# The first modulated norm in four blocks instead of two, and ten row tiles of the fourth modulation segment on ScalarE and GpSimd instead of six of the third on VectorE

## What is computed

```python
silu_c = jax.nn.silu(c)                                   # c: (1, 2048)
mod = silu_c @ w_ada[l] + b_ada[l]                        # w_ada: 2048 x 12288
shift_m, scale_m, gate_m, shift_f, scale_f, gate_f = jnp.split(mod, N_MOD, axis=-1)
h = modulate(rmsnorm(x, g_norm_mix[l]), shift_m, scale_m) # h * (1 + scale) + shift
proj = h @ w_in[l]                                        # queries, keys, values, latents
dq, dk, dv, q_lat, kv_lat, k_pe = jnp.split(proj, IN_SPLITS, axis=-1)
```

## Time and profile before

| | |
|---|---|
| median of 3 runs | 2601.45 us (2601.24 to 2601.49) |
| time of the profiled execution | 2600.53 us |
| its span | 2598.9 us |
| TensorE busy | 2526.1 us, 97% |
| VectorE busy | 1936.0 us, 74% |
| ScalarE busy | 1135.2 us, 44% |
| GpSimd busy | 175.8 us, 7% |
| chain that ended last | TensorE 80%, VectorE 8%, DMA 6%, issue 2%, ScalarE 2% |
| mean DMA rate | 253 GB/s |
| slices 1 to 3 of 40 (65 us each) | TensorE 5, 9, 9 tenths busy; 374, 370, 364 GB/s |

### The profile page before, as it was taken

How to read it: one execution, slowest core, us unless ns; L and a number is a source line. 1 busy time by engine, 2 the same in 40 slices (tenths; PEclk the granted TensorE clock), 3 DMA queues, 4 the chain that set the end, 5 groups by cost and what they waited for, 6 DMA issues and landing times.

```text
span 2598.9 us, 45233 instructions
## 1 busy us (share of the span) xinstructions
PE 2526.1 (97%) x17210; PEld 2274.1 (88%) x17210; DVE 1936.0 (74%) x2037; ACT 1135.2 (44%) x1326; POOL 175.8 (7%) x288
## 2 busy tenths in 40 slices
PE   5999999999999999999999999999989999999998
PEld 3787789788999998998999999999969898898986
DVE  2476598778788887889878988888777566575665
ACT  2334444444444444444334444544454444444443
POOL 6000000200001010110000000001010000000000
PEclk8999999999999999999999999999999999999999
DMA  9998868688889887886877765678847676676764
GB/s 374 370 364 291 268 216 291 203 284 303 291 291 311 287 297 252 303 300 194 265 219 235 235 219 158 186 246 280 284 141 254 207 241 226 212 246 211 225 219 138
DMA packets 304432, 658.63 MB, mean 253 GB/s; under 512 B 31351, under 2 KB 37646, under 8 KB 303918
## 3 DMA queue, kind: packets, MB, share of 16 engines
q1 hardware_dynamic: 271376, 538.12, 61.0%
q0 software_dynamic: 32480, 117.56, 13.7%
q10 hardware_dynamic: 446, 1.13, 0.1%
HBM read 654.62 MB, written 2.10 MB: 253 GB/s over the span
## 4 chain that ended last, share of the span: by engine, by line
PE 80%; DVE 8%; DMA 6%; issue 2%; ACT 2%; SPq 0%; ACTq 0%; DVEq 0%
PE ps L2106 19%; PE ps L2107 10%; PE ps L2077 9%; PE ps L2078 9%; PE ps L2079 9%; PE ps L2154 6%; PE ps L2156 6%; PE ps L2155 6%; DMA raw<-in_w_ff 3%; DVE lo L1161 3%; DMA proj<-in_w_ada 1%; DMA raw<-in_w_in 1%; DVE work L1186 1%; ACT hi L717 1%; PE ps L2323 1%
## 5 line engine op out<-in xcount | busy, mean ns | idle before, releaser
L1161 DVE TENSOR_TENSOR lo<-raw,hi 128x1024 fp32r<-128x1024 f32 (+2 forms) x868 | 1036.8, 1210 | 516.5 <-ACT hi L717 513.4
L717 ACT ACTIVATE hi<-raw 128x1024 fp32r<-128x1024 f32 (+2 forms) x868 | 901.6, 1049 | 1166.0 <-PE ps L2079 391.9
L2106 PE MATMUL ps<-acts,hi 128*128 128x512 f32 x2048 | 673.9, 383 | 9.1 <-DVE lo L1161 6.7
L2077 PE MATMUL ps<-acts,hi 128*128 128x256 f32 x2384 | 668.4, 280 | 9.2 <-issue 2.7
L2078 PE MATMUL ps<-acts,hi 128*128 128x256 f32 x2384 | 658.8, 276 | 0.0
L2079 PE MATMUL ps<-acts,lo 128*128 128x256 f32 x2384 | 658.8, 276 | 0.0
L2107 PE MATMUL ps<-acts,lo 128*128 128x256 f32 x2048 | 558.7, 273 | 0.0
L2077 PEld LDWEIGHTS ps<-acts,hi 128*128 128x128 f32 x2384 | 458.6, 192 | 41.2 <-issue 33.7
L2078 PEld LDWEIGHTS ps<-acts,hi 128*128 128x128 f32 x2384 | 458.7, 192 | 0.7 <-issue 0.2
L2079 PEld LDWEIGHTS ps<-acts,lo 128*128 128x128 f32 x2384 | 458.9, 192 | 0.2
L2106 PEld LDWEIGHTS ps<-acts,hi 128*128 128x128 f32 x2048 | 387.3, 189 | 67.3 <-DVE lo L1161 9.5
(11 more groups left out here) (308 smaller groups left out, 2437.2 us busy)
## 6 DMA issues: line engine op xcount, KB each, us to landing
raw<-in_w_ff SPq DMA_DIRECT2D x512, 512.0 KB, 4.7
raw<-in_w_in SPq DMA_DIRECT2D x232, 512.0 KB, 4.6
ada_ring<-in_w_ada POOLq DMA_DIRECT2D x150, 512.0 KB, 5.4
proj<-in_w_ada SPq DMA_DIRECT2D x92, 512.0 KB, 8.3
proj<-in_w_ada POOLq DMA_DIRECT2D x64, 512.0 KB, 5.3
ada_ring<-in_w_ada SPq DMA_DIRECT2D x40, 512.0 KB, 6.5
raw<-in_w_out SPq DMA_DIRECT2D x32, 512.0 KB, 5.6
raw<-in_w_o SPq DMA_DIRECT2D x32, 512.0 KB, 5.6
```

What stands on the lines that cost most here:

```text
L717: nc.scalar.activation(hi[n % SPLIT][:, 0:k], raw[n % RAW][:, 0:k], ACT.Copy).then_inc(hi_ready, 1)
L1161: V.tensor_tensor(lo[n % SPLIT][:, 0:k], raw[n % RAW][:, 0:k], hi[n % SPLIT][:, 0:k].bitcast(F32), ALU.subtract)\
L2077: M(out, h, right_hi, start=start, stop=False)
L2106: M(out[:, j, :], h[:, t, js], both, start=k == 0, stop=False)
```

## The change

`BLOCKS` and `OPEN` become 4. A block is now 512 columns of the shift and of the scale together, 8 block tiles, each of which brings 512 columns of both segments; `turn_block` makes both at once with two-column matmuls, and `finish_block` writes both. Only block 0 stands ahead of the first chunk. Each block has 8 chunks: four groups of 512 columns, with two chunks (4 k tiles) each. A group's partial sum leaves PSUM after its two chunks: VectorE copies it into `proj` in block 0 (L1521) and adds it there in the others (L1524), 16 passes of 128x1024. The 8 tiles of the next block stand behind the chunks 0 to 4 of a block, its turn behind chunk 5.

22 pairs are left, between chunks 24 and 62: all of segment 2, and the last 6 row tiles of segment 3. The first ten row tiles of segment 3 come as twenty halves. Each is loaded behind chunk 37 + h, scaled in place by ScalarE behind the split that stands at chunk 33 + h, and added by GpSimd. The load of half h waits until half h - 4 was added. `sum_halves` stands in `kvlat`. Rotations of keys and queries are cut differently: two of 4 tiles and one of 2 in `qk1`, three of 2 in `v1` (before: three of 4 and two of 2).

```diff
-OPEN = 3
-BLOCKS = 2
+OPEN = 4
+BLOCKS = 4
-HALVES = 12
+HALVES = 20
...
-        tiles_after = {1: (0,), 2: (1, 2), 3: (3,), 4: (4, 5), 5: (6,), 6: (7, 8), 7: (9, 10), 8: (11, 12), 9: (13, 14, 15)}
-        half_lo = (16, 18, 19, 21, 22, 24, 29, 30, 32, 33, 34, 35)
+        tiles_after = {0: (0, 1), 1: (2,), 2: (3, 4), 3: (5,), 4: (6, 7)}
+        TURN_AFTER = 5
+        pair_after = {(24 + 21 * p // 15 if p < KT else 47 + 15 * (p - KT) // (KT - MOVED - 1)): p for p in range(2 * KT - MOVED)}
+        halves_after = {33 + h: (h,) for h in range(HALVES)}
...
@@ SyncE
-                    sp.dma_start(start_ring[n % START][t], w_ada[0][row:row + P, col:col + 2 * NC]).then_inc(start_landed[n % START], 16)
+                    both = w_ada[0][row:row + P, 0:2 * D].rearrange("p (s n) -> p s n", s=2)[:, :, b * NC:(b + 1) * NC]
+                    sp.dma_start(start_ring[u % START][t].rearrange("p (s n) -> p s n", s=2), both).then_inc(start_landed[u % START], 16)
...
@@ GpSimd, behind the rotation tables
+            for h in range(ADA, HALVES):
+                part = half_sum[h % ADA]
+                pool.wait_ge(half_scaled, h - ADA + 1)
+                pool.wait_ge(half_used, max(ADA, h - 1))
+                nc.gpsimd.tensor_tensor(part, part, half_tiles[h % RING], ALU.add).then_inc(half_used, 1)
...
@@ ScalarE
+            for n in range(SPLIT):
+                split_chunk(n)
             norm_root()
...
+            for n in range(STARTED):
+                b, i = n // PER_BLOCK, n % PER_BLOCK
+                split_chunk(n + SPLIT)
+                if b + 1 < BLOCKS:
+                    if i == TURN_AFTER - 1:
+                        copy_block(b + 1)
+                    if i == TURN_AFTER:
+                        act.wait_ge(mods_block, b + 2)
+                        block_hi(b + 1, 0)
+                    if i == TURN_AFTER + 1:
+                        block_hi(b + 1, 1)
...
+                    nc.scalar.activation(tile, tile, ACT.Copy, scale=col).then_inc(half_scaled, 1)
...
@@ VectorE
-                    V.scalar_tensor_tensor(part, tile, col, part, ALU.mult, ALU.add).then_inc(half_used, 1)
+            for n in range(STARTED):
+                b, i = n // PER_BLOCK, n % PER_BLOCK
+                split_chunk(n + SPLIT)
+                if n % PER_GROUP == PER_GROUP - 1:
+                    partial_sum(n // PER_GROUP)
+                if b + 1 < BLOCKS:
+                    if i == TURN_AFTER:
+                        finish_block(b + 1)
+                        block_normed(b + 1)
+                    if i == TURN_AFTER + 1:
+                        block_low(b + 1, 0)
+                        block_low(b + 1, 1)
...
@@ TensorE
+            for u in range(TILES):
+                block_tile(u)
+                if u == START - 1:
+                    spread_sum("mix")
+            turn_block(0)
             pe.wait_ge(lam_ready, 1)
+            for n in range(STARTED):
+                b, i = n // PER_BLOCK, n % PER_BLOCK
+                start_chunk(n)
+                if b + 1 < BLOCKS:
+                    for m in tiles_after.get(i, ()):
+                        block_tile(TILES * (b + 1) + m)
+                    if i == TURN_AFTER:
+                        turn_block(b + 1)
```

More of the change, by code:

```diff
@@ L505, in start_chunk @@
             def start_chunk(n):
[L507 to L525, removed]
+                b, g, c = n // PER_BLOCK, n % PER_BLOCK // PER_GROUP, n % PER_GROUP
+                k, col = BLOCK_KT * b + CK * c, COLUMN_BLOCK[g] * NC
+                chunk(n, 0, (slot(n), w[:, k:k + CK, col:col + NC]))
+            for u in range(START):
+                block_tile(u)
+            for n in range(STARTED):
+                start_chunk(n)
+                for u in tiles_issued.get(n, ()):
+                    block_tile(u)
             groups(first["v1"][0], 0, w, 4 * NC, FULL)
@@ L915, in diff_step, with scaled_half, with_halves @@
                 return hooks
+            def scaled_half(h):
+                tile, col = half_tiles[h % RING], silu[:, h // ADA:h // ADA + 1]
+                act.wait_ge(half_landed[h % RING], 16 * (h // RING + 1))
+                if h < ADA:
+                    nc.scalar.activation(half_sum[h], tile, ACT.Copy, scale=col).then_inc(half_used, 1)
+                else:
+                    nc.scalar.activation(tile, tile, ACT.Copy, scale=col).then_inc(half_scaled, 1)
+            def with_halves(phase, hooks, c0=0):
+                for c in range(FULL):
+                    for h in halves_after.get(first[phase][0] + c0 + c, ()):
+                        step = hooks.get(c)
+                        hooks[c] = lambda h=h, step=step: (step and step(), scaled_half(h))
+                return hooks
             def copy_sums(*segs):
@@ L1508, in _, with rope_half @@
+            def rope_half(tile):
+                rope(proj[:, tile:tile + 2, :], cos_d, sin_d, 7)
             finish_block(0)
             block_normed(0)
-            for b in range(BLOCKS):
-                n0 = PER_BLOCK * b
-                finish_block(2 * b + 1)
-                for c in range(4):
-                    split_chunk(n0 + c)
-                    block_low(b, c)
-                for j in range(4, PER_BLOCK):
-                    split_chunk(n0 + j)
-                    if n0 + j in half_lo:
-                        ada_half(half_lo.index(n0 + j))
-                    if b == 0 and j == 9:
-                        finish_block(2)
-                        block_normed(1)
@@ L1539, in _ @@
-            group(FIRST, OPEN, out=plain(proj[:, DQ + 4 * OPEN:DQ + 4 * OPEN + 4, :]),
-                  after={c: lambda c=c: rope_or_half(c) for c in range(FULL)})
+            block_low(0, 0)
+            block_low(0, 1)
+            for n in range(STARTED):
[10 more added lines that the diff above has]
+                        block_low(b + 1, 1)
+                if n == STARTED - 6:
+                    dve.wait_ge(sin_ready, 1)
+                    rope(proj[:, DQ:DQ + 4, :], cos_d, sin_d)
+                if n == STARTED - 4:
+                    rope(proj[:, DK:DK + 4, :], cos_d, sin_d)
+                if n == STARTED - 2:
+                    rope_half(DQ + 4)
```

264 lines of the change are left out of this document (120 added, 144 removed).

## The result

The changed kernel takes **2617.24 us** (median of 4, 2614.09 to 2618.81) against 2601.47 us of the kernel before, measured beside it: ratio **1.0067**, 95% interval 1.0051 to 1.0082 (the two medians alone give 1.0061). The forecast was 2596.4. The profiled execution took 2614.09 us, 13.6 more than the one of before. There are four sessions, so some differences between ratios go across two of them. The interval of each ratio is 2.3 to 4.2 us to either side.

A forecast was written before the change was run, and what follows sets the result against it. TensorE was taken as the bound, with DMA nearly level in the 32 chunks. -17.8 + 13.1 - 2.05 + 1.7 = -5.05 us against 2601.45 gave 2596.4; its own range 2593 to 2600, with rivals 2586 to 2605.

The forecast's parts named there:

- Step 3: From `v1` to `kvlat`: fewer pairs -4.0 us, half a rotation turn +0.95, longer wait in `kvlat` +1.0; sum -2.05 us.
- Both are hidden.: ScalarE's 20 added passes (21 us, in `v1`) and VectorE's 16 partial sums (20 us, in the earlier stretch) cost no time.
- the first rival: Same as "GpSimd's adds set the pace": slower, 2607.5 us, chance 0.16.
- In `v1` TensorE has no idle time: Sign to check in `v1`: any idle time of TensorE there would make the prediction wrong by that amount.
- GpSimd's adds set the pace: 18 adds at up to 5.0 us delay loads and chunks, deciding from about 4.4 us; 2607.5 us, chance 0.16.
- Step 1: Start-up: fewer tiles ahead of chunk 0, which starts at 46.4 us against 64.14, -17.8 us.
- Step 2: The 32 chunks take 136.9 us, +13.1, including TensorE waits of 2.8 us at each of three block borders.
- Step 4: TensorE's clock falls behind one in three border waits: +1.7 us, bounds 0 and 5.1.
- Free border: Rival: norm passes finish sooner, so no border waits or clock falls; tile 31 then decides; 2587.3 us, chance 0.22.

## Why the prediction was wrong

- **Step 3 failed: "Both are hidden."** The sum of -2.05 is right for a kernel without the adds (178.5 against 178.1). I had set the scalings against the idle time of ScalarE and the passes against that of VectorE; the adds had no term of their own outside the first rival. What they cost lies in VectorE's passes, which are held in a chain that TensorE waits for in program order: 19.0 us (197.5 against 178.5 without adds). 12.8 of these are waits of TensorE (14.6 against 1.8 between 189 and 335 us); the falls of the clock behind them are the likely rest. "In `v1` TensorE has no idle time" was the sign that showed it in the trace: 14.4 us of idle time ahead of the turns between 189 and 335, and two clock falls.
- **The rival "GpSimd's adds set the pace"** had the right engine and the wrong mechanism. The adds take 2.4 to 3.5 us, below its 4.4, and GpSimd idles between them. SyncE does wait for adds, nine times and 18.3 us in all between 185 and 345, but no split waits for a chunk of `w_in` there. The earlier trace rows showed the contention: the 0.83 beside an add, where two passes take 0.87 together. I read it as a lower rate of GpSimd and multiplied by the size, where the question was who stands still for how long, and who waits for the one that stands. The Trainium skill has the rule (SBUF — State Buffer, Who interferes with whom): VectorE and GpSimd share a pair of ports by an exclusive lock, which VectorE needs for two inputs in SBUF or in a mode that uses two ports, and the one that comes second is blocked for the whole instruction of the other. The page cited in the prediction says only that they contend. The trace agrees with the lock: 2.14 us for a 128x4 pass, and 1.03 when the add is cut in two; the reciprocal, with one input in SBUF, is not held (0.16).
- **Step 1** was 2.65 us short (49.05 against 46.4; its terms as listed add up to 46.0 only). Tile 7 is used 1.5 later (40.47; its place in the ring of six comes free only when TensorE has used tile 1, at about 28), and its matmuls take 1.94 at half clock, not 1.1. Most of the rest is the time to the second `block_low` pass, 1.4 for 0.9, beside GpSimd's work on the angles (four passes in 2.56).
- **Step 2** held. Waits of 2.59 against 2.8, three of three. The stretch took 139.9 us; steps 2 and 4 gave 136.9 and 1.7 for it. Removing the waits gave back 8.3 us. The sum of the three is 7.8; two falls of the clock went with them, and two waits for tiles (1.08 and 1.49) came.
- **Step 4** counted one fall and two came in the 32 chunks, 0.91 granted in 84:104 and in 144:164. Over the eight kernels with these border waits, 10 of 24 waits cost the clock, so one in three was near. The two behind the waits in `v1` and later belong to step 3.
- **"Free border"**: its premise (the passes get through sooner) is not met as the kernel stands. With VectorE's order changed and the adds gone, it gives 0.9959, 2590.8 us (2587.4 to 2594.4); the rival said 2587.3, and named tile 31 as the next limit. A wait of 1.82 us does stand ahead of tile 31 in that run; that it is what limits the gain is not shown.
- With the adds off GpSimd, the rest of the change gives 2599.4 (0.9992, fused passes on VectorE), 3 us over the forecast. The shortfall of step 1 is of that size, and so is the interval.

## What to carry to other kernels

Before work goes to GpSimd because it is idle, look up what VectorE does in the same microseconds and who waits for it: beside a chain of short VectorE passes without slack, GpSimd's adds on SBUF made the chain longer; beside passes with some chunks to spare they cost little. The same ten adds cost 9.9 us more in one place than in another. And when a wait stands at a border, list what the engine does ahead of the pass that is waited for: here two passes that nobody needed yet stood first.

## What the runs showed of the hardware

- Where both work on SBUF, VectorE and GpSimd alternated by whole instructions. A 128x4 pass took 2.14 us beside adds of 128x1024 and 1.03 beside adds of 128x512; an add was held in turn (3.48 against 2.38 us). Cutting the instruction left the time as it was (1.0059 against 1.0067), since more passes are held, each for less.
- VectorE's passes that read PSUM were not held: 0.68 us for L1417 in the middle of an add, and 1.22 for the reduction that starts at 230.61, inside the add of 229.02. Nor was the reciprocal, which reads one tile of SBUF (0.16), while a TENSOR_SCALAR of 128x256 that also reads one tile of SBUF was (2.40 against 0.35). Why some are spared was not tried.
- A wait of 2.6 us cost the clock in two places of three, and the later ones of 5.0 and 5.6 us in both. In the eight kernels with the same three waits, the granted clock shows a fall behind 10 of 24: the same wait at the same place costs it in some traces and not in others.
